# Two attentions of a decoder trunk: mask products ahead of the score products, and scores cut into 128-column pieces

## The reference, cut to what matters

```python
# sparse attention (256 tokens: selection and window both reduce to the causal mask)
s_s = jnp.einsum('bqkgd,bqknjd->bqkgnj', qrb, k_sel) * scale
m_s = tok <= t[None, :, None, None, None]
p_s = masked_softmax(s_s, m_s[:, :, :, None], axis=(-2, -1))
...
s_w = jnp.einsum('bqkgd,bwkd->bqkgw', qrb, kwb) * scale
p_w = masked_softmax(s_w, m_w[None, :, None, None, :])
o = gb[..., 0:1] * o_c + gb[..., 1:2] * o_s + gb[..., 2:3] * o_w
...
# differential attention
s = jnp.einsum('bqhcd,bkhcd->bhcqk', qb, k) * scale
mask = kpos[None, :] <= t[:, None]
p = masked_softmax(s, mask[None, None, None])
a = p[:, :, 0] - lam * p[:, :, 1]
return jnp.einsum('bhqk,bkhd->bqhd', a.astype(v.dtype), v)
```

## Time and profile before

| | |
|---|---|
| Median of 3 runs | 646.2 us (646.13 to 646.63) |
| The profiled execution's own time | 646.59 us |
| Its span in the trace | 644.8 us |
| TensorE busy | 630.0 us, 98% of the span |
| VectorE busy | 526.0 us, 82% |
| ScalarE busy | 417.9 us, 65% |
| Mean granted TensorE clock | 0.994 of full speed |

### The profile page before, as it was taken

One profiled execution on the slowest core, in us unless ns is written; L12 is line 12 of the kernel. 1 busy time (PEld: TensorE's weight loads), 2 busy tenths in 40 slices (PEclk: granted clock), 3 DMA queues, 4 the chain that ended last, 5 costly groups with the idle time before them and its releaser, 6 DMA issues.

```text
span 644.8 us, 10731 instructions
## 1 busy us (share of the span) xinstructions
PE 630.0 (98%) x3614; PEld 528.9 (82%) x3614; DVE 526.0 (82%) x942; ACT 417.9 (65%) x817; POOL 41.9 (6%) x101
## 2 busy tenths in 40 slices
PE   9999989999999999999999999989999999999995
PEld 8998766678888888888887888768988888888894
DVE  4588687857999988888888556877899898888887
ACT  6554577847766666666667464884866666666666
POOL 1100023400000000000012000150000000000000
PEclk9999999999999999999999999989999999999998
DMA  8777050034465555555515544703455555555521
GB/s 313 267 252 277 1 197 2 2 131 163 164 212 188 194 191 196 196 196 196 196 66 196 204 166 170 261 18 127 168 196 197 196 196 189 190 187 192 186 70 66
DMA packets 21456, 109.11 MB, mean 169 GB/s; under 512 B 2608, under 2 KB 2992, under 8 KB 12464
## 3 DMA queue, kind: packets, MB, share of 16 engines
q1 hardware_dynamic: 21136, 108.48, 47.4%
q10 hardware_dynamic: 288, 0.22, 0.1%
HBM read 107.64 MB, written 1.05 MB: 169 GB/s over the span
## 4 chain that ended last, share of the span: by engine, by line
PE 87%; DVE 8%; ACT 2%; issue 1%; DMA 1%; SPq 0%; DVEq 0%; ACTq 0%
PE psU L674 21%; PE psA L463 13%; PE psA L464 13%; PE psA L465 13%; PE psU L679 10%; PE psU L900 2%; PE psA L860 1%; PE psU L885 1%; DVE arena L1819 1%; PE psU L474 1%; DVE arena L2108 1%; PE psU L654 1%; PE psU L653 1%; PE psU L652 1%; DMA stage<-in_w_group 1%
## 5 line engine op out<-in xcount | busy, mean ns | idle before, releaser
L674 PE MATMUL psU<-hA,win_hi 128*128 128x512 f32 x608 | 190.8, 395 | 0.0
L679 PEld LDWEIGHTS psU<-hA,win_lo 128*128 128x128 f32 x608 | 114.2, 188 | 26.6
L679 PE MATMUL psU<-hA,win_lo 128*128 128x256 f32 x608 | 119.4, 278 | 0.0
L1793 DVE TENSOR_TENSOR win_lo<-stage,win_hi 128x1024 fp32r<-128x1024 f32 x86 | 104.9, 1221 | 0.0
L674 PEld LDWEIGHTS psU<-hA,win_hi 128*128 128x128 f32 x608 | 95.3, 189 | 2.8
L1291 ACT ACTIVATE win_hi<-stage 128x1024 fp32r<-128x1024 f32 x89 | 93.3, 1051 | 5.6 <-PE psA L465 5.6
L1819 DVE SCALAR_TENSOR_TENSOR arena<-arena,prm 128x255 f32<-128x255 f32 (+1 forms) x168 | 77.3, 481 | 3.7 <-ACT arena L1303 0.7
L1701 DVE TENSOR_TENSOR win_lo<-stage,win_hi 128x1024 fp32r<-128x1024 f32 (+3 forms) x50 | 55.8, 1153 | 14.6 <-ACT win_hi L1219 14.4
L463 PE MATMUL psA<-wout_hi,act_hi 128*128 128x512 f32 x168 | 65.9, 393 | 0.3
L464 PE MATMUL psA<-wout_lo,act_hi 128*128 128x512 f32 x168 | 65.5, 390 | 0.0
L465 PE MATMUL psA<-wout_hi,act_lo 128*128 128x512 f32 x168 | 65.4, 389 | 0.0
(11 more groups left out here) (315 smaller groups left out, 1135.5 us busy)
## 6 DMA issues: line engine op xcount, KB each, us to landing
stage<-in_w_ffn_in SPq DMA_DIRECT2D x44, 1024.0 KB, 4.8
stage_out<-in_w_ffn_out SPq DMA_DIRECT2D x44, 516.0 KB, 5.0
stage<-in_w_kv SPq DMA_DIRECT2D x8, 1024.0 KB, 4.9
stage<-in_w_dq SPq DMA_DIRECT2D x4, 1024.0 KB, 4.8
stage<-in_w_dout SPq DMA_DIRECT2D x4, 1024.0 KB, 4.9
stage<-in_w_group SPq DMA_DIRECT2D x3, 1024.0 KB, 5.0
stage<-in_w_nsa_out SPq DMA_DIRECT2D x3, 1024.0 KB, 4.8
stage<-in_w_phi SPq DMA_DIRECT2D x2, 1024.0 KB, 5.9
```

What stands on the lines that cost most here:

```text
L674: mm(o, win_hi[:, slot, cs], hA[:, k, :, :].rearrange("p a q -> p (a q)"), start=k == 0, stop=False)
L679: last = mm(o[:, 0:S], win_lo[:, slot, cs], hA_hi[:, k2, :], start=False, stop=k2 == KT - 1)
L1793: last = dve.tensor_tensor(win_lo[:, win, cs], stage[:, slot, cs], win_hi[:, win, cs].bitcast(F32), sub)
```

## The change

The mask products become the first ones of a unit: they open both banks (`start=True`), and the score products add to them. In the sparse attention they get a function of their own, `nsa_mask(u)`, which takes the wait for free banks with it and is called one trip ahead: `nsa_mask(u + 3)` directly behind the turns of unit u. In the differential attention they stand directly ahead of the unit's score products. The score products are cut into pieces of 128 columns (`b`), so that a `t = 1` unit has 8 in place of 4, and the two heads alternate inside; the last score product now lets VectorE go on.

```diff
--- before.py
+++ after.py
@@ -840,9 +840,9 @@
 
             UNITS = [(g, t, m2) for g in range(KVH) for t in range(TT) for m2 in range(2)]
 
-            def nsa_scores(u):
-                g, t, m2 = UNITS[u]
-                m, nk = 2 * g + m2, (t + 1) * P
+            def nsa_mask(u):
+
+                t = UNITS[u][1]
                 if u < 2:
 
                     pe_.wait_ge(sem["proj_act"], NG - 1 + u)
@@ -851,17 +851,21 @@
 
                     pe_.wait_ge(sem["negmax"], u - 1)
                     pe_.wait_ge(sem["probs"], 4 * (u - 1))
-
+                for e in range(2):
+                    bank = psA[:, 2 * (u % 2) + e, :].rearrange("p (y k) -> p y k", y=2)
+                    mm(bank[:, :, t * P:(t + 1) * P], identb[:, :], cmask2, start=True, stop=False)
+
+            def nsa_scores(u):
+                g, t, m2 = UNITS[u]
+                m = 2 * g + m2
                 pe_.wait_ge(sem[("kT_act", "kT_dve")[g % 2]], 2 * (g // 2 + 1))
                 for y in range(2):
-                    for e in range(2):
-                        rows = slice(e * 64, e * 64 + 64)
-                        k0 = g * 512 + y * S
-                        mm(psA[:, 2 * (u % 2) + e, y * S:y * S + nk], qrT[rows, m, t * P:(t + 1) * P], keysT[rows, k0:k0 + nk],
-                           start=y == 0, stop=False)
-                for e in range(2):
-                    bank = psA[:, 2 * (u % 2) + e, :].rearrange("p (y k) -> p y k", y=2)
-                    last = mm(bank[:, :, t * P:nk], identb[:, :], cmask2, start=False, stop=True)
+                    for b in range(t + 1):
+                        for e in range(2):
+                            rows = slice(e * 64, e * 64 + 64)
+                            k0 = y * S + b * P
+                            last = mm(psA[:, 2 * (u % 2) + e, k0:k0 + P], qrT[rows, m, t * P:(t + 1) * P],
+                                      keysT[rows, g * 512 + k0:g * 512 + k0 + P], start=False, stop=y == 1 and b == t)
                 last.then_inc(sem["scores"], 1)
 
             def act_copies(n):
@@ -937,12 +941,15 @@
             pe_.wait_ge(sem["phi_k_in"], 64)
             pe_.wait_ge(sem["phi_v_in"], 64)
             phi_half(1, phi_k1, phi_v1)
+            nsa_mask(0)
+            nsa_mask(1)
             nsa_scores(0)
             nsa_scores(1)
             for v in range(2):
                 pe_.wait_ge(stage_full[v], 16 * loads_of(N_A - 2 + v))
             phi_half(0, stage[:, 0, :], stage[:, 1, :])
             nsa_transpose(0)
+            nsa_mask(2)
             nsa_scores(2)
             nsa_transpose(1)
 
@@ -950,6 +957,7 @@
             for c in range(2):
                 last = pe_.transpose(psO[:, 1, 0:256].rearrange("p (v c x) -> p c v x", v=2, c=2)[:, c], hid[:, c * P:(c + 1) * P], ident[:, :])
             last.then_inc(sem["hidT_bank"], 1)
+            nsa_mask(3)
             nsa_scores(3)
 
             pe_.wait_ge(sem["params_in"], 16)
@@ -969,12 +977,15 @@
                               w2[:, 1, c, 0:HD], start=c == 0, stop=c == 1)
             last.then_inc(sem["vcmp_bank"], 1)
             cmp_scores()
+            nsa_mask(4)
             nsa_scores(4)
             nsa_transpose(2)
+            nsa_mask(5)
             pe_.wait_ge(sem["cmp_shift"], 1)
             nsa_pv(0, 0)
             nsa_scores(5)
             nsa_transpose(3)
+            nsa_mask(6)
 
             for u in range(4, len(UNITS)):
                 if u + 2 < len(UNITS):
@@ -989,6 +1000,8 @@
                                                  cmp_p[:, t, 8 * b:8 * b + 8, :].rearrange("p h c -> p (h c)"), ident[:, :])
                     last.then_inc(sem["cmpT_bank"], 1)
                 nsa_transpose(u)
+                if u + 3 < len(UNITS):
+                    nsa_mask(u + 3)
                 if u == 4:
                     pe_.wait_ge(sem["cmpT_ready"], 1)
                     nsa_pv(0, 1)
@@ -1044,15 +1057,16 @@
                 if u >= 4:
                     pe_.wait_ge(sem["dnegmax"], d_maxima(u - 1))
                     pe_.wait_ge(sem["dprobs"], 4 * (u - 1))
+                for c in range(2):
+                    bank = banks[:, c, :].rearrange("p (e k) -> p e k", e=2)
+                    mm(bank[:, :, t * P:nk], identb[:, :], cmask2, start=True, stop=False)
                 for e in range(2):
                     h = 2 * hp + e
-                    for c in range(2):
-                        rows = slice(c * 64, c * 64 + 64)
-                        mm(banks[:, c, e * S:e * S + nk], qrT[rows, h, t * P:(t + 1) * P], keysT[rows, h * S:h * S + nk],
-                           start=e == 0, stop=False)
-                for c in range(2):
-                    bank = banks[:, c, :].rearrange("p (e k) -> p e k", e=2)
-                    last = mm(bank[:, :, t * P:nk], identb[:, :], cmask2, start=False, stop=True)
+                    for b in range(t + 1):
+                        for c in range(2):
+                            rows = slice(c * 64, c * 64 + 64)
+                            last = mm(banks[:, c, e * S + b * P:e * S + (b + 1) * P], qrT[rows, h, t * P:(t + 1) * P],
+                                      keysT[rows, h * S + b * P:h * S + (b + 1) * P], start=False, stop=e == 1 and b == t)
                 last.then_inc(sem["dscores"], 1)
 
             for g in range(6):
```

## The result

| | before | after |
|---|---|---|
| median | 646.2 us (15 runs, 645.9 to 646.88) | 647.83 us (15 runs, 646.93 to 648.83) |
| profiled execution, its span | 646.59 us, 644.8 us | 647.49 us, 645.7 us |
| TensorE, VectorE, ScalarE busy | 630.0, 526.0, 417.9 us | 628.9, 526.3, 417.3 us |

The ratio is 1.0022, 95% interval 1.0014 to 1.0029: slower by 0.9 to 1.9 us. The range of 645.6 to 648.6 us holds it; the forecast of 647.1 us is 0.7 us too low, and the time lies just beyond the 0.2% up to which I called a change no change. So the case that came is "slower", to which I gave 0.34, and not "no change" with 0.54.

A forecast was written before the change was run, and what follows sets the result against it. TensorE, 87% of the span, was taken as the bound, in the sparse attention from 96.2 us. Start +0.37, loop +0.36 and differential attention +0.25 gave +0.98 us; forecast 646.2 + 0.9 = 647.1 us, range 645.6 to 648.6.

The forecast's parts named there:

- The start: Sparse attention, 74 to 96 us: mask products first delay unit 0's release by 0.24, unit 3 adds 0.13; sum +0.37 us.
- The loop: Sparse attention, 96 to 125 us: pairs moved behind the turns, split units and one added wait; sum +0.36 us.
- Pair behind the turns: Sparse loop, units 7 to 15: each of nine mask pairs costs 0.22 us behind the turns, +1.98 us.
- split: Score products cut to 128 columns: +0.03 us for each t = 1 unit, +0.15 us for five in the loop.
- eight-turn trips: Sparse loop trips with eight turns: taking away the mask pair ahead gives back 0.28 and 0.34 us, twice each.
- With the semaphore's way that is +0.15 us: Sparse loop, trip of u = 5: the moved mask pair waits for unit 6's exponentials, +0.15 us.
- The differential units 0 to 2: Differential attention in the TensorE-bound projection: units 0 and 1 +0.13 us together, unit 2 +0.10 us.
- The differential units behind them: Differential attention from unit 3: unit 3 +0.02 us, then VectorE and ScalarE carry the chain, so nothing more.
- The loop goes by the release: Faster rival: score release, not TensorE's length, sets the loop; earlier release gives -1.4, 644.8 us; chance 0.15.
- The moved wait: Slower rival: exponentials late for the mask pair in four loop trips, 0.35 us each, 648.4 us; chance 0.17.
- The passes: Slower rival: TensorE does not keep 57 ns a score pass over sixteen; at 65 ns 648.1 us; chance 0.08.
- The clock: Rival: the half-clock stretch, 428.60 to 432.00 us, goes (up to 1.7 us back, 645.4) or another comes (648.8); chance 0.06.

The follow-up runs named there:

- g_start_trip5: Changed kernel with unit 0's mask and scores ahead of unit 1's, and unit 8's mask pair directly ahead of its scores: 647.33 us against 646.30 for the kernel before.
- e_trip5_late: Changed kernel with unit 8's mask pair issued one trip later, directly ahead of its scores: 647.21 us, ratio 1.0018 to the kernel before.
- f_after_fill: Changed kernel plus 15 unread mask products in two TensorE waits at the differential attention's end: 647.38 us, ratio 1.0013 to the kernel before.
- i_after_units3: Changed kernel with the 15 filling products, differential units 3 to 7 in the old order: 646.74 us against 646.53 for the kernel before.
- e_diff_only: Changed kernel with the sparse attention of before, so only the differential attention changed: 646.76 us against 646.06 for the kernel before.
- e_sparse_only: Changed kernel with the differential attention of before, so only the sparse attention changed: 647.35 us against 646.06 for the kernel before.
- f_before_fill: Kernel before plus 15 unread mask products in two TensorE waits at the differential attention's end: 645.82 us against 646.30 for the kernel before.

## Why the prediction was right in its parts and short in its sum

**The start: right.** +0.37 forecast, +0.34 measured. VectorE reads unit 0's maxima 0.24 us later, as the sum had it (1.69 us behind the last product ahead, 76.16 - 74.47, in place of 75.58 - 74.13 = 1.45). g_start_trip5 gives back 0.22 of it (+0.12).

**The loop: right in its terms, but for the wait.** Pair behind the turns 0.22 us (0.81 us for turns and pair, as worked out), split +0.03 a unit, eight-turn trips 1.24 us. The step that failed in size is "With the semaphore's way that is +0.15 us": it is 0.34 us in the profile of after. I let unit 6's exponentials end with the last ACTIVATE of the earlier trace rows and left out the read of the row sum behind it (+0.09 us), whose semaphore is the one that the mask pair waits for; and from that read's end at 101.39 to the first mask product at 101.53 it is 0.14 us, where I had allowed 0.04. Together that is the 0.19 us by which the loop is longer than forecast. e_trip5_late, without the wait, has +0.35, of which some 0.1 is the pair that it places between two changes of shape; the other terms so come to 0.21 to 0.25 us, forecast 0.21.

**The differential units 0 to 2: right.** +0.23 forecast, +0.23 measured.

**The differential units behind them: wrong.** "Behind that VectorE and ScalarE carry the chain" put the moved pairs of units 4 to 7 at nothing. The chains of the kernels with the old order bear the sentence out; with the changed order it no longer holds. From unit 3's mask to its turns, 7 us on, the chain of f_after_fill stays on TensorE, pair, pieces and value products in a row; the turns of unit 3 come 0.23 us later, and they hold ScalarE's exponentials and, behind these, its squares and GpSimd's scaling of the heads, by 0.14 us; GpSimd's first steps, falling into VectorE's instruction, add 0.13. The part of the differential attention that I put at +0.02 us costs 0.27 - 0.05 = 0.22. TensorE waits for that scaling at the very end; the changed kernel's timeline:

```profile
433.86 1.07 PE L594 MATMUL psA<-wout_hi,hB_lo 128*128 128x512 f32 x4
435.31 0.66 PE L1128 MATMUL psU<-ident,tokB 128*128 128x128 f32 x4 [0.38 <-POOL tokB L330]
```

i_after_units3 shows the place (0.3 us gone with units 3 to 7 as before); that the way there is the one named rests on the chains alone. The profile of before could not show it: its low clock held TensorE back until GpSimd was done, so no wait for GpSimd stood there. I had read a disturbed stretch as the kernel's own.

**Total.** Without low clock in either kernel: 0.34 + 0.55 + 0.23 - 0.05 + 0.27 = 1.34 us (0.27 being -0.56 less the -0.83 of the two kernels with an unchanged end). Forecast 0.98, of which I added 0.9 to the median. The measured difference of the medians is 1.6 us. The mean clock that comes with each execution falls into two groups, up to 0.994 and from 0.995; among the profiles, those up to 0.994 hold the stretch. By that, executions without it have medians of 647.28 after (7) and 645.93 to 646.09 before (the four sets beside the experiments, 45 executions): 1.2 to 1.35 us, the size of the stretches' sum. That they meet so closely is partly luck. The same comparison of executions from 0.995 on gives +0.31 us for e_diff_only (3 executions), +0.52 for e_sparse_only (5), +0.33 for g_start_trip5 (5) and +1.14 for e_trip5_late (7), where the stretches add up to 0.43, 0.90, 0.95 and 1.11; groups this small carry the scatter of the first loads. So the single terms are shown by the stretches, and by the medians only that the change costs some 1 to 2 us. Those with the stretch have 648.08 (8) and 646.34 to 646.72 (63), 1.4 to 1.7 us apart. Why the low clock costs the changed kernel 0.8 us and the kernel before 0.4 to 0.7 is open; no run was made for it.

**The rivals.** *The loop goes by the release* did not come: L867 holds VectorE for 4.8 us where L864 did for 4.6. *The moved wait* came in one trip with the 0.35 us that the rival asked for, not in four: lateness did not come round again, the trips of u = 4 and 8 have none, and that of u = 9 has 0.03 us. *The passes* take 1.09 us for sixteen to the next shape and 0.65 for eight, so (1.09 - 0.65) / 4 = 0.11 us a pair, and that rival falls. The Trainium skill's 62 ns a product without hardware decoding ("TensorE: Matmul & The Clock Gate", section "Wait — 56ns, not 53.3ns?") is not what bounds them over sixteen passes either; by that rule, as an estimate, they would have taken 0.1 us more. *The clock* was priced wrong: "if the stretch goes, up to 1.7 us come back". It went in f_before_fill. The end is 0.81 us shorter in that profile, and the medians fell by 0.5 us (645.82 and 645.85 against 646.30 and 646.41), about half of the executions beside them having had no such stretch to lose. It is not 1.7 us because behind TensorE GpSimd's scaling is next: it ends at 433.85 us in f_before_fill and TensorE goes on at 433.91., read for TensorE alone, did not say so.

**Left open.** Whether the mask pair first with uncut score products would save the 0.03 us a unit wasn't tried. The kernel before with the filling products is the fastest seen here, by 0.5 us in two sets, and each interval ends at about 1. A version between the two kernels that would take most of the change's cost away, g_start_trip5 with units 3 to 7 as before, wasn't run.

## What to carry to other kernels

A product that is moved to a place where its engine is alone on the path costs its full pitch there, and what it leaves behind is only what it did not hide: here nine pairs cost about as much behind the turns as they gave back ahead of them. Before a dependency is moved, read what raises its semaphore: a sum taken along with an activation is ready one instruction later. And look at the granted clock before calling a stretch's order of waits the kernel's own, since a slowed engine hides the wait that stands next.

## What the runs showed of the hardware

An exponential with a row sum is two rows of ScalarE, and the second one, the read of the sum, raises the semaphore. It takes 0.23 us and ended 0.09 us behind the ACTIVATE (101.39 against 101.30); the product that waited for it started 0.14 us later.

The low clock of 3.4 us behind two TensorE waits of 0.8 and 1.2 us came in some executions of one and the same program and not in others: by their mean clocks in 63 of the 108 of the kernel before, and in none of the 66 in which fifteen filling products stood in those waits. The waits alone do not settle whether it comes: e_sparse_only, whose differential attention is that of the kernel before, has the same waits of 0.8 and 1.2 us in its profile, at full clock.

GpSimd's steps on 128 x 4 elements take 0.20 to 0.24 us each with 0.07 to 0.09 us between them, seventeen of them 5 us of a chain that TensorE ends up waiting for. Longer ones, of 0.28 to 0.40 us, come only beside the instructions with which VectorE mixes the probabilities in SBUF: in all 14 profiles each of them starts while such an instruction runs and ends 0.06 to 0.08 us behind it. Steps that start beside VectorE's copies and maxima out of PSUM keep 0.20 us. It goes the other way as well: the mixing instruction beside GpSimd's scaling of 1.04 us (L330) takes 1.18 to 1.36 us, the next one 0.47. This is why the first step of the second chain took 0.20 us with the old differential order and 0.35 to 0.39 with the changed one, where it comes 0.14 to 0.18 us after the start of VectorE's instruction.
